# Loading the down weights of an expert pair ahead of the gate and up weights of the next pair

## The reference

```python
D_MODEL, N_EXPERTS, EXPERT_FF = 1024, 32, 256

def _moe(h, w_rg, b_rg, w_re, b_re, w_eg, w_eu, w_ed):
    ...
    for g in range(N_GROUPS):
        sl = slice(g * EXPERTS_PER_GROUP, (g + 1) * EXPERTS_PER_GROUP)
        a = jnp.einsum('nd,edf->nef', hf, w_eg[sl])
        u = jnp.einsum('nd,edf->nef', hf, w_eu[sl])
        act = jax.nn.silu(a) * u * combine[:, sl, None]
        out = out + jnp.einsum('nef,efd->nd', act, w_ed[sl])
    return out.reshape(lead + (D_MODEL,))
```

## Time and profile before

| | us |
|---|---|
| median of 3 runs | 925.07 |
| lowest, highest of the 3 | 924.95, 929.11 |
| time of the profiled execution | 924.58 |
| its span, from the first to the last instruction | 922.7 |
| PE busy | 747.7 (81%) |
| DVE busy | 353.5 (38%) |
| ACT busy | 271.3 (29%) |
| POOL busy | 87.2 (9%) |

### The profile page before, as it was taken

How to read it: one execution, slowest core, us unless ns; L and a number is a source line. 1 busy time by engine, 2 the same in 40 slices (tenths; PEclk the granted TensorE clock), 3 DMA queues, 4 the chain that set the end, 5 groups by cost and what they waited for, 6 DMA issues and landing times.

```text
span 922.7 us, 12174 instructions
## 1 busy us (share of the span) xinstructions
PE 747.7 (81%) x5071; PEld 552.9 (60%) x5071; DVE 353.5 (38%) x617; ACT 271.3 (29%) x499; POOL 87.2 (9%) x133
## 2 busy tenths in 40 slices
PE   0698799988988999899999899725998778788820
PEld 0588799765788999777999877513442223233310
DVE  1562545365456532734355522463110111011036
ACT  4313513244476654233322222310110101001014
POOL 3103000000000010100000000011112112121214
PEclk9999789899999999999999999865998989899975
DMA  8332021111311253343132269551899999999652
GB/s 272 112 112 95 1 92 46 46 46 47 92 46 46 83 199 109 134 141 114 51 86 73 90 238 389 232 207 37 344 423 422 423 423 424 423 410 407 281 199 105
DMA packets 74135, 173.50 MB, mean 188 GB/s; under 512 B 6944, under 2 KB 41984, under 8 KB 65744
## 3 DMA queue, kind: packets, MB, share of 16 engines
q1 hardware_dynamic: 65040, 151.46, 43.5%
q0 software_dynamic: 9040, 21.26, 6.6%
HBM read 163.75 MB, written 18.74 MB: 198 GB/s over the span
## 4 chain that ended last, share of the span: by engine, by line
PE 53%; DMA 17%; DVE 12%; ACT 7%; issue 4%; SPq 2%; POOL 0%; POOLq 0%; ACTq 0%; DVEq 0%
PE bank L672 31%; DMA expert_down<-in_w_exp_down 12%; PE bank L1072 6%; PE bank L1088 4%; DMA expert_gate_up<-in_w_exp_up 2%; SPq L494 2%; DMA w_raw<-in_w_in 2%; PE bank L692 1%; DVE s_state L1641 1%; DVE token_out L1877 1%; DVE w_split L1400 1%; ACT w_split L1118 1%; ACT scores L1219 1%; PE bank L876 1%; PE bank L1011 1%
## 5 line engine op out<-in xcount | busy, mean ns | idle before, releaser
L672 PE MATMUL bank<-hT_split,w_split 128*128 128x272 f32 x1200 | 163.7, 295 | 3.5 <-DVE w_split L1400 1.4
L672 PEld LDWEIGHTS bank<-hT_split,w_split 128*128 128x128 f32 x1200 | 156.8, 193 | 6.5 <-issue 3.4
L672 PE MATMUL bank<-w_split,hT_split 128*128 128x512 f32 (+1 forms) x576 | 131.6, 382 | 0.0
L1072 PE MATMUL bank<-expert_gate_up,gatheredT 128*64 128x512 f32 x512 | 115.3, 603 | 5.2 <-DMA expert_gate_up<-in_w_exp_up 4.4
L672 PEld LDWEIGHTS bank<-w_split,hT_split 128*128 128x128 f32 x576 | 100.6, 190 | 23.4 <-issue 4.3
L1400 DVE TENSOR_TENSOR w_split<-w_raw,w_split 128x2048 fp32r<-128x2048 f32 (+2 forms) x36 | 77.1, 2142 | 87.6 <-ACT w_split L1118 87.6
L1088 PE MATMUL bank<-expert_down,expert_actT 128*64 128x512 f32 x256 | 70.1, 698 | 34.4 <-DMA expert_down<-in_w_exp_down 30.4
L1072 PEld LDWEIGHTS bank<-expert_gate_up,gatheredT 128*64 128x64 f32 x512 | 39.5, 139 | 78.6 <-issue 75.0
L1118 ACT ACTIVATE w_split<-w_raw 128x2048 fp32r<-128x2048 f32 (+2 forms) x36 | 64.4, 1788 | 62.8 <-DMA w_raw<-in_w_in 29.7
L1088 PEld LDWEIGHTS bank<-expert_down,expert_actT 128*64 128x64 f32 x256 | 21.1, 158 | 72.8 <-issue 40.2
L1854 DVE TENSOR_TENSOR expert_act<-expert_silu,bank 128x256 f32<-128x256 f32 x16 | 6.7, 421 | 113.8 <-ACT expert_silu L1343 113.8
(11 more groups left out here) (339 smaller groups left out, 926.9 us busy)
## 6 DMA issues: line engine op xcount, KB each, us to landing
expert_gate_up<-in_w_exp_gate SPq DMA_DIRECT2D x32, 1024.0 KB, 18.7
expert_gate_up<-in_w_exp_up SPq DMA_DIRECT2D x32, 1024.0 KB, 20.9
expert_down<-in_w_exp_down SPq DMA_DIRECT2D x32, 1024.0 KB, 20.3
w_raw<-in_w_in SPq DMA_DIRECT2D x15, 1024.0 KB, 5.0
w_raw<-in_w_in SPq DMA_DIRECT2D x17, 512.0 KB, 4.3
s_state<-in_state_gla POOLq DMA_DIRECT2D x4, 1024.0 KB, 10.0
out_sample_gla_state<-s_state POOLq DMA_DIRECT2D x4, 1024.0 KB, 7.2
w_raw<-in_w_proj_gla SPq DMA_DIRECT2D x8, 512.0 KB, 4.4
```

The costliest lines, as they stand in the source:

```text
L672: ins = mm(out, stat(x, k), mov(y, k), start=first and n == 0 and m == 0, stop=last and n == len(ks) - 1 and m == 2)
L1072: ins = mm(P[2 + u][64 * half:64 * half + 64, :].rearrange("p (m n) -> p m n", m=2), XT[u][:, k, 64 * half:64 * half + 64], WGU[gb][:, hal ...
```

## The change

In the written-out loop the two halves of the body change places. Down of pair n now stands ahead of gate and up of pair n + 1 in SP's queue, each with its own wait. The loads before that loop, the run-time loop behind it, the waits' values and all other engines stay as they are.

```diff
             for n in range(2, 2 * PEELED):
+                sp.wait_ge(dn_done, n - 1)
+                load_down(n % 2, pair(n))
                 if n + 1 < 2 * PEELED:
                     sp.wait_ge(gu_done, n - 1)
                     load_gate_up((n + 1) % 3, pair(n + 1))
-                sp.wait_ge(dn_done, n - 1)
-                load_down(n % 2, pair(n))
             sp.wait_ge(iters_ready, 2)
```

## The result

| | before | after |
|---|---|---|
| median, us | 926.07 (6 runs) | 932.6 (6 runs) |
| lowest, highest, us | 924.95, 929.48 | 931.11, 934.51 |
| profiled execution, us | 924.58 | 931.54 |
| its span, us | 922.7 | 929.7 |

The changed kernel is slower. The ratio is 1.0064 with a 95% interval of 1.004 to 1.0088, which is 5.9 us of 926 (3.7 to 8.1). This interval holds the forecast's 5.6 us, but also the 4.0 of the recovered start, and the 8.1 of the slow last block stands at its edge. Which of them came true has to be read from the traces.

The account below looks back on a forecast made before the run. The prediction took one stream of DMA transfers in the expert stage as the bound. A stream start 5.59 us later, all else at zero, gave 925.07 + 5.59 = 930.7 us, with a range of 928.0 to 934.0.

Parts of the forecast that it names:

- the recovered start: Rival: shortfalls at 820 to 835 us and the stream's first slices are cured; +4.0 us, 929.1; chance 0.24.
- the slow last block: Rival: pair 15's gate and up matmuls run on the slow clock, up to 2.51 us more, up to 933.2; chance 0.2.
- The bound: Expert stage: one stream of transfers on busy DMA engines sets the time; 30.4 us of down waits move, not gained.
- The first load, +5.59 us: Start of the loop: SP's first load is issued at 653.72 instead of 648.13, so the stream starts 5.59 us later.
- The stream stays full: Loop after its first load: the queue doesn't run dry at the waits for dn_done; cost zero.
- The dry stream: Rival: the queue empties at waits for dn_done, up to 1.5 us each; one or two give 932 to 934; chance 0.05.
- The handover: Passage to the run-time loop, 820 to 835 us: at best 1.2 us of rate shortfall comes back; not in the sum.
- The tail: Behind the last gate and up weights: 7.09 us of matmuls and the rest unchanged; only PE's clock may move.
- A slow start behind every wait: Skill's rule for PE bursts behind DMA waits: by it the last block is slow too, sum 8.1 us.

Follow-up runs that it names:

- experiment 3: Kernel before, with the new order of loads only from n = 4 on, the first two turns of the loop in the old order: ratio 1.0006, no difference.
- experiment 1: Kernel before, with the new order at the first turn of the loop alone (n = 2): ratio 1.0066, 6.1 us slower.
- experiment 2: Kernel before in the old order, with only the loop's first load also waiting for the first down matmuls (dn_done 1): ratio 1.0082, 7.6 us slower.
- experiment 4: Kernel before, with the new order from n = 3 on and the old order at the first turn: ratio 1.0003, not told from no change.
- Experiment 5: Kernel before in the old order, with the loop's first load waiting for gu_done 2 instead of 1: ratio 1.0109, 10.1 us slower.
- 9: Kernel before plus spare matmuls, pair 0's gate and up buffer released by halves, and the new order from n = 4 on: ratio 0.9953, 4.4 us faster.
- 6: Kernel before in the old order, with pair 0's gate and up buffer released and reloaded by halves: ratio 0.9983, 1.6 us faster.
- second run of 8: Kernel before in the old order, with spare matmuls and pair 0's gate and up buffer released by halves, run again: ratio 0.995, 4.6 us faster.

## Why the prediction was right, point by point

- **The bound.** The prediction took the stream as the bound and the down waits as its shadow. This was right: the waits moved to the other weights, the share stayed at 1.02, and experiment 3 changed the waits without changing the time.
- **The first load, +5.59 us.** The issue moved by 5.60 us and the time by 5.9 (3.7 to 8.1). The time alone would fit the recovered start and hardly exclude the slow last block; the later issue and pair 15's start, 5.3 us later and without a slow block, are what tells them apart. Experiments 1 and 2 show it from both sides, by the first exchange alone and by the delay without any exchange.
- **The stream stays full.** It did. The issue at `dn_done` of pair 1, at 668.21, found work in the queue: the share is 0.93 or more in each microsecond from 667 to 673. The time from first issue to pair 15 is that of before. PE was held from pair 4's gate and up block on (a wait of 1.54 us), a pair earlier than I wrote, which cost nothing. The dry stream, given 0.05, needs the exchange at the second turn without the one at the first (experiment 4), where it cost a gap of 0.8 us.
- **The handover.** The shortfall did vanish: 421 GB/s from 826 to 841 us, where it was 389 from 820 to 835. But the gain of 1.2 us did not come. From first issue to pair 14's block are 861.73 - 655.76 = 205.97 us, against 854.38 - 648.13 = 206.25 before, so 0.3 us of it. That I left it out of the sum was right. That I put 0.24 on a rival built from it was too much. Experiment 3, where PE waited for pair 15's weights in the new order, has 221.15 us instead of 221.57, so 0.4. And yet the mean rate is 422 instead of 419 GB/s over the 210 us, worth 1.5 us by this estimate. The end of the stream fits engines that finish unevenly: the share falls from 0.99 to 0.29 within 4 us before (864 to 868) and from 0.93 to 0.27 within 6 us after (870 to 876). A mean over 16 engines isn't what a landing waits for, but which engine lands last was not measured.
- **The tail.** The rival of the slow last block was built on a wait that decides at about 3.1 us. That point was wrong, and the trace of the kernel before could have told. There a wait of 3.10 us was followed by a fast block and two shorter ones by slow blocks:

```profile
721.05 5.35 PE L1088 MATMUL bank<-expert_down,expert_actT 128*64 128x512 f32 x16 [3.09 <-DMA expert_down<-in_w_exp_down]
...
819.86 5.35 PE L1088 MATMUL bank<-expert_down,expert_actT 128*64 128x512 f32 x16 [2.51 <-DMA expert_down<-in_w_exp_down]
```

In the changed kernel waits of 2.48 and 2.67 us were followed by slow blocks, and the wait of 2.64 us ahead of pair 15 was followed by 7.09 us in the kernel before and by 8.78 in experiment 1. What PE did earlier differs between the two: ahead of pair 14 it had waited 1.72 us before and 2.88 us in experiment 1. Experiment 5 (1.52, then 2.62) was fast and experiment 2 (2.98, then 2.63) slow, which fits, but no run tests it. In all four profiles whose last turns are in the new order (the changed kernel and experiments 3, 4 and 9) the slow block fell on pair 14, where it took the place of pair 15's wait and added nothing. In experiments 1, 2, 6 and the second run of 8 it fell on pair 15 and added 1.7 us. In the old order it comes and goes, so it belongs in the range, as it was. That the changed kernel was spared it is luck in part: the prediction had only given it a chance.

- **A slow start behind every wait.** The Trainium skill ("TensorE: Matmul & The Clock Gate", section "HAM oscillation — how this bites in real kernels") has a kernel in which every burst behind a DMA wait of about 3 to 5 us starts on the throttled clock. The trace of the changed kernel agrees for its five gate and up waits of 3.44 us and more, whose blocks were all slow. Of the shorter ones those of 2.67 and 2.48 us were followed by slow blocks too and those of 1.72, 1.71, 1.54 and 1.03 us were not. The last block, for which the prediction used the rule, had no wait ahead of it.
- **The number.** 930.7 was worked out from a median of 925.07 and measured as 932.6 beside a median of 926.07. About 1 us of the difference is the kernel before itself in more runs, the rest is within the interval. That 932.6 lies near the 933.2 of the slow last block says nothing for it, since the last block was fast in the profiled execution; the other executions have no trace.

## What to carry to other kernels

When the transfer engines are busy without a gap, the order of the queue only chooses which weight the compute engine waits for; what still moves the end is when the stream starts and how well its bytes move. So look at the first load behind a full set of buffers: a wait put ahead of it for a buffer it doesn't need costs about its length (5.6 us of wait, 5.9 us of time here), though the same exchange in the later turns made no difference that could be measured. To gain, free the first buffer sooner, even by means that look unrelated, such as spare matmuls that have the clock up by then (2.7 us here).

## What was not expected of the hardware

- The same wait of 2.64 us ahead of the same 32 matmuls was followed by 7.09 us in one kernel and 8.78 us in another. The length of that wait alone didn't tell which.
- Reloading a 4 MiB buffer in two halves ran at 318 and 330 GB/s with the engines' share at 1.06 and 0.95, against 415 and 393 GB/s for whole loads. Pieces of 4 KB are not slow by themselves: those of the down weights moved at 418 GB/s. The slow stretch (242 GB/s at a share of 1.00 from 651 to 655 us) came with the second half, and its cause is open. A share near 1 doesn't mean the full rate.
- A delay of 12.4 us cost 10.1 us (6.5 to 13.7), and in the profiles the stream behind it was 2.3 us shorter. By the estimate above 1.25 us of that is traffic of gathers and scatters that got done ahead of the stream, and the rest was not found.
